# Convolution products moved from GpSimd to ScalarE, and two ScalarE steps placed one ring step sooner

## The reference, cut to what matters

```python
h = rmsnorm(x, norm_mix_pre)
proj = h @ w_in
xr, yr, q, k, v, g_rnn, g_attn = jnp.split(proj, IN_OFFSETS, axis=-1)
# causal depthwise convolution, CONV_WIDTH = 4
xp = jnp.pad(xr, ((0, 0), (3, 0), (0, 0)))
y = conv_b
for k in range(4):
    y = y + xp[:, k:k + S] * conv_w[k]
# recurrence, in 8 blocks of 256 features
r = sigmoid(einsum(y, w_rg_a) + b_rg_a)
i = sigmoid(einsum(y, w_rg_x) + b_rg_x)
log_a = -8.0 * r * softplus(-lru_lambda)
a, mult = exp(log_a), sqrt(-expm1(2.0 * log_a))
h_t = a * h_(t-1) + mult * (i * y)      # an associative scan over time
y_rnn = h * gelu(yr)
y_att = sliding_window_sink_attention(rope(q), rope(k), v, sinks)
```

## Time and profile before

| | |
|---|---|
| median of 3 runs | 2308.87 us (2307.55 to 2314.53) |
| the profiled execution | 2309.7 us, its span 2308.0 us |
| mean granted PE clock | 0.995 of 2.4 GHz |
| PE busy | 2253.3 us, 98% of the span |
| DVE, ACT, POOL busy | 62%, 52%, 17% |

### The profile page before, as it was taken

One profiled execution on the slowest core, in us unless ns is written; L12 is line 12 of the kernel. 1 busy time (PEld: TensorE's weight loads), 2 busy tenths in 40 slices (PEclk: granted clock), 3 DMA queues, 4 the chain that ended last, 5 costly groups with the idle time before them and its releaser, 6 DMA issues.

```text
span 2308.0 us, 32955 instructions
## 1 busy us (share of the span) xinstructions
PE 2253.3 (98%) x11754; PEld 1896.5 (82%) x11754; DVE 1431.4 (62%) x1625; ACT 1195.7 (52%) x1850; POOL 382.0 (17%) x408
## 2 busy tenths in 40 slices
PE   7999999999999999999999999999999999999999
PEld 6888899788888778888888888888977778888887
DVE  6666666654554465555555555566899977675554
ACT  5554456644444446555555555555444446554442
POOL 2134430000000102122121211211233311110000
PEclk9999999999999999999999999999999999999999
DMA  8544444566666856666666666665656665556655
GB/s 246 165 136 136 139 145 147 177 189 192 190 191 193 263 172 188 194 206 203 195 206 204 195 207 199 200 200 163 194 185 187 186 182 166 166 163 191 188 187 163
DMA packets 215028, 427.01 MB, mean 185 GB/s; under 512 B 14033, under 2 KB 14321, under 8 KB 214385
## 3 DMA queue, kind: packets, MB, share of 16 engines
q1 hardware_dynamic: 206720, 398.51, 56.5%
q0 software_dynamic: 7744, 26.62, 3.7%
q10 hardware_dynamic: 432, 0.13, 0.0%
HBM read 414.71 MB, written 10.49 MB: 184 GB/s over the span
## 4 chain that ended last, share of the span: by engine, by line
PE 81%; DVE 11%; ACT 3%; issue 3%; DMA 2%; POOL 1%; SPq 0%; ACTq 0%; DVEq 0%
PE acc L1855 23%; PE acc L1857 22%; PE acc L1856 22%; DVE w_lo L1149 3%; PE acc L1847 3%; PE acc L1849 3%; PE acc L1850 3%; PE tps L1870 1%; DMA raw<-in_w_out_dram 1%; DMA raw<-in_w_in_dram 1%; ACT w_hi L660 1%; POOL k_t L577 1%; PE tps L1976 1%; PE sides L1976 1%; PE sides L1926 1%
## 5 line engine op out<-in xcount | busy, mean ns | idle before, releaser
L1149 DVE TENSOR_TENSOR w_lo<-raw,w_hi 128x1024 fp32r<-128x1024 f32 x752 | 941.4, 1256 | 764.0 <-ACT w_hi L660 759.8
L660 ACT ACTIVATE w_hi<-raw 128x1024 fp32r<-128x1024 f32 x752 | 794.1, 1059 | 904.1 <-PE acc L1857 739.7
L1855 PE MATMUL acc<-w_hi,h_hi 128*128 128x512 f32 x1440 | 572.5, 398 | 5.8 <-DVE w_lo L1149 5.8
L1857 PE MATMUL acc<-w_hi,h_lo 128*128 128x512 f32 x1440 | 562.5, 391 | 0.0
L1856 PE MATMUL acc<-w_lo,h_hi 128*128 128x512 f32 x1440 | 561.8, 390 | 0.0
L1855 PEld LDWEIGHTS acc<-w_hi,h_hi 128*128 128x128 f32 x1440 | 270.7, 188 | 73.1 <-issue 16.8
L1857 PEld LDWEIGHTS acc<-w_hi,h_lo 128*128 128x128 f32 x1440 | 270.6, 188 | 57.4
L1856 PEld LDWEIGHTS acc<-w_lo,h_hi 128*128 128x128 f32 x1440 | 271.1, 188 | 52.9
L1855 PE MATMUL acc<-w_hi,slab_dg_r 128*128 128x512 f32 x768 | 300.5, 391 | 3.6 <-DVE w_lo L1149 3.6
L1856 PE MATMUL acc<-w_lo,slab_dg_r 128*128 128x512 f32 x768 | 299.9, 390 | 0.0
L1857 PE MATMUL acc<-w_hi,slab_dg_r 128*128 128x512 f32 x768 | 299.8, 390 | 0.0
(11 more groups left out here) (370 smaller groups left out, 2314.6 us busy)
## 6 DMA issues: line engine op xcount, KB each, us to landing
raw<-in_w_in_dram SPq DMA_DIRECT2D x328, 512.0 KB, 3.8
raw<-in_w_mlp_up_dram SPq DMA_DIRECT2D x128, 512.0 KB, 3.8
raw<-in_w_mlp_down_dram SPq DMA_DIRECT2D x128, 512.0 KB, 4.7
raw<-in_w_out_dram SPq DMA_DIRECT2D x64, 512.0 KB, 4.6
raw<-in_w_rnn_proj_dram SPq DMA_DIRECT2D x32, 512.0 KB, 3.9
raw<-in_w_attn_proj_dram SPq DMA_DIRECT2D x32, 512.0 KB, 4.8
trig_scratch<-tmp POOLq DMA_DIRECT2D x32, 256.0 KB, 4.4
raw<-in_w_proj_ssm_dram SPq DMA_DIRECT2D x16, 512.0 KB, 3.8
```

Source lines behind the costliest of these rows:

```text
L660: nc.scalar.activation(w_hi[:, j % RING], raw[:, j % RING], ACT.Copy).then_inc(hi_ready, 1)
L1149: V.tensor_tensor(w_lo[:, j % RING], raw[:, j % RING], w_hi[:, j % RING].bitcast(F32), ALU.subtract)\
L1855: T.matmul(o, hi[:, k, c], wh, start=first, stop=False)
L1857: ins = T.matmul(o, lo[:, k, c], wh, start=False, stop=last)
```

## The change

Three things change.

1. ACT makes the scaled copies. A new function `conv_taps(k)` on ACT makes four copies of 128x256 elements per tap, at steps 8, 10, 13 and 13 (`TAPS_AT`) of the attention tables, behind `y_hi` of the same step. Tap 3 writes `slab_d` with the bias, taps 2, 1 and 0 write three buffers `taps[k]`. POOL keeps only the three sums (`conv_sum`).
2. `load_rg(1)` is issued after the last convolution, since its buffers now hold taps until then. `load_rg(0)` stays where it was.
3. In the gelu units ACT's `gates` moves from step 2 to 1 and `decays` from step 3 to 2.

```diff
-        tap = slab_e[:, 8:12, :]
+        taps = [slab_i[:, 12:16, :], slab_e[:, 12:16, :], slab_e[:, 8:12, :]]
...
-                    def conv(c, k):
...
-                        late = 3 - k
-                        if k == 3:
-                            for m in range(QPC):
...
-                                chain.mark(pool.tensor_scalar(slab_d[:, at, :], xr_c[:, m, :], w, b, ALU.mult, ALU.add))
-                            chain.wait()
-                            return
...
-                        chain.link(pool.tensor_tensor(tap[:, :, late:], xr_c[:, :, 0:SEQ - late], w, ALU.mult))
-                        o = slab_d[:, c * QPC:(c + 1) * QPC, late:]
-                        ins = pool.tensor_tensor(o, o, tap[:, :, late:], ALU.add)
+                    def conv_sum(c, k):
+
+                        pool.wait_ge(tap_ready, 4 * c + 4 - k)
+                        o = slab_d[:, c * QPC:(c + 1) * QPC, 3 - k:]
+                        ins = pool.tensor_tensor(o, o, taps[k][:, :, 3 - k:], ALU.add)
...
                     load_rg(0)
-                    pool.wait_ge(tps_ready, NH)
-                    load_rg(1)
-
                     pool.sem_inc(conv_ready, 1)
                     for c in range(NH):
                         normalise(None, c, 0)
                         normalise(None, c, 1)
-                        pool.wait_ge(acc_free[0], c + 2)
-                        conv(c, 3)
                         normalise(None, c, 2)
                         normalise(None, c, 3)
-                        conv(c, 2)
-                        conv(c, 1)
-                        conv(c, 0)
+                        for k in (2, 1, 0):
+                            conv_sum(c, k)
+                    pool.wait_ge(conv_ready, NH + 1)
+                    load_rg(1)
...
+        TAPS_AT = [8, 10, 13, 13]
...
+                def conv_taps(k):
+
+                    if k == 3:
+                        act.wait_ge(acc_free[0], lin(i, 1, c + 2))
+                        act.wait_ge(conv_ready, lin(i, 1, c + 1))
+                    for m in range(QPC):
+                        w = pt1[:, span(i, QPC, COL1["conv_w"] + KT * k + QPC * c + m)]
+                        if k == 3:
+                            b = pt1[:, span(i, QPC, COL1["conv_b"] + QPC * c + m)]
+                            ins = nc.scalar.activation(slab_d[:, span(i, QPC, QPC * c + m), :].rearrange("p o c -> p (o c)"),
+                                                       xr_c[:, m, :], ACT.Identity, scale=w, bias=b)
+                        else:
+                            ins = nc.scalar.activation(taps[k][:, m, 3 - k:], xr_c[:, m, 0:SEQ - 3 + k], ACT.Copy, scale=w)
+                    ins.then_inc(tap_ready, 1)
...
-                return {0: [lambda: gelu(c)], 2: [lambda: gates(c)], 3: [lambda: decays(c)], 4: [lambda: root(c)], 7: [lambda: y_high(c)]}
+                return {0: [lambda: gelu(c)], 1: [lambda: gates(c)], 2: [lambda: decays(c)], 4: [lambda: root(c)], 7: [lambda: y_high(c)]}
```

More of the change, by code:

```diff
@@ L203, in griffin_block_then_ssm_block @@
         conv_ready, rg_done, w_ready = sem("conv_ready"), sem("rg_done"), sem("w_ready")
-        xc_read = sem("xc_read")
+        xc_read, tap_ready = sem("xc_read"), sem("tap_ready")
         d_ready, root_ready, y_ready = sem("d_ready"), sem("root_ready"), sem("y_ready")
@@ L502, in normalise @@
                         ins.then_inc(norm_ready, 1)
-                    def conv(c, k):
-                        late = 3 - k
-                        if k == 3:
-                            for m in range(QPC):
-                                at = c * QPC + m
-                                w = pt1[:, COL1["conv_w"] + KT * k + at:COL1["conv_w"] + KT * k + at + 1]
-                                b = pt1[:, COL1["conv_b"] + at:COL1["conv_b"] + at + 1]
-                                chain.mark(pool.tensor_scalar(slab_d[:, at, :], xr_c[:, m, :], w, b, ALU.mult, ALU.add))
-                            chain.wait()
-                            return
-                        at = COL1["conv_w"] + KT * k + c * QPC
-                        w = pt1[:, at:at + QPC].unsqueeze(2).broadcast_to([P, QPC, SEQ - late])
-                        chain.link(pool.tensor_tensor(tap[:, :, late:], xr_c[:, :, 0:SEQ - late], w, ALU.mult))
-                        o = slab_d[:, c * QPC:(c + 1) * QPC, late:]
-                        ins = pool.tensor_tensor(o, o, tap[:, :, late:], ALU.add)
+                    def conv_sum(c, k):
+                        pool.wait_ge(tap_ready, 4 * c + 4 - k)
+                        o = slab_d[:, c * QPC:(c + 1) * QPC, 3 - k:]
+                        ins = pool.tensor_tensor(o, o, taps[k][:, :, 3 - k:], ALU.add)
                         if k:
@@ L794, in attention @@
                     places += [(at + 1, lambda p=p: exps(p)), (Y_ATT_AT[p] - 1, lambda p=p: pt_copy(p)), (Y_ATT_AT[p], lambda p=p: y_hi(p))]
+                places += [(at, lambda k=k: conv_taps(k)) for at, k in zip(TAPS_AT, (3, 2, 1, 0))]
                 return placed(places, S, 2)[0]
```

## The result

| | before | after |
|---|---|---|
| median of 4 runs | 2309.23 us (2307.55 to 2314.53) | 2291.72 us (2290.99 to 2294.39) |
| the profiled execution | 2309.7 us, span 2308.0 | 2291.69 us, span 2290.0 |

The ratio is 0.9925, with a 95% interval from 0.9911 to 0.9939. The kernel became 17.5 us faster, and the forecast of 2292 us holds. That the medians agree to 0.3 us is partly luck: the changed kernel measured once more, beside the kernel before, was 16.4 us faster.

A forecast was written before the change was run, and what follows sets the result against it. PE, busy 98%, was taken as the bound, losing time to waits on DVE and a slow clock behind them. 12.2 + 4.5 = 16.7 us off 2309.7 gives 2293.0, on the median's scale 2292 us, range 2289 to 2295 (70%).

The forecast's parts named there:

- The rotation: Turn of q after blocks' convolutions: PE's three waits for DVE's last sum (7.3 us) and slow clock (4.9) go, -12.2 us.
- the two meetings of 0.86 us: POOL's three sums behind the last `normalise`: two meet DVE's `w_lo`, each 0.86 us longer, so they end at 123.8 us.
- The spare time: Rotation done at 126.8 us, PE arriving at 128.0 us: PE does not wait, with 1.2 us to spare.
- slow clock: Turn to scores behind each rotation wait: excess of 1.54, 1.72 and 1.63 us at reduced PE clock, 4.9 us in all.
- The gelu and mix units: Earlier gates and decays remove PE's waits for `w_lo` in three gelu units and the first mix unit: -4.5 us.
- the 1.7 us gone in the mix unit: First mix unit: DVE's `decay` starts 1.7 us sooner, so PE's 1.7 us wait for `w_lo` goes.
- the wait goes, in three units: 2.8 us: Gelu units: PE's 0.9 us wait for `w_lo` disappears in each of three units, 2.8 us in all.
- The late load: `load_rg(1)` moved from the start to about 305 us: nothing won at the start, cost 0.
- ACT's copies: 16 copies per block at 0.5 us, 32 us in all on ACT: cost nothing, `pt_copy` done at 118.6 us, covered by 1.3.
- The late rotation: Rival, 15%: POOL's sums still hold DVE's rotation, 1 us of waiting and 1.6 us slow clock three times: 2300 us.
- The gelu rival: Rival, 7%: gelu units win nothing, as the late split of step 3 makes its `w_lo` the next wait: 2296 us.
- its edge of 0.67 us a copy: Rival, 4%: ACT too slow; above 0.67 us a copy, each 0.1 us costs 3.2 us; at 1.5 us, 2319 us.

The follow-up runs named there:

- The kernels with short waits: The changed kernel plus one or two POOL subtractions that read SBUF behind each block's last sum: 2292.30 us with one, 2294.48 us with two.
- its own experiment: The kernel before with only `load_rg(1)` moved behind the last convolution: 2307.83 us, ratio 0.9996 (0.9987 to 1.0006).
- the first reordered kernel: The kernel before with the new gelu places, convolution whole on POOL, taps 3 and 2 ahead of the third `normalise`, tap 1 ahead of the fourth: 2299.93 us.
- part 1 alone: The changed kernel with `gates` and `decays` put back at steps 2 and 3: 2297.09 us, ratio 0.9952 (0.9936 to 0.9969).

## Why the prediction was right, step by step

**The rotation: 12.5 us, forecast 12.2.** The bound was read rightly: DVE's sums were held by POOL's reads, and the experiment with writes against those with reads shows it. The Trainium skill ("SBUF — State Buffer", section "Who interferes with whom") says that a DVE instruction with two SBUF inputs contends with a GpSimd instruction that reads SBUF and not with one that only writes. The runs agree in both halves: 0.42 us beside 5.01 us of memsets, 2.10 us beside a read.

Each time of the working can be checked, with the 0.40 us added by which this trace is early. POOL's sums end at 123.8 (forecast 123.8 to 124.1), with the two meetings of 0.86 us. The first rotation sum is not held, where up to 0.4 us was allowed. The rotation ends at 126.4 (forecast 126.8). PE arrives at 128.04 (forecast 128.0), both counted from the end of its last matmul. The spare time is 1.6 us, not 1.2.

The split between wait and slow clock was not quite right. The excess of 1.54 and 1.72 us from turn to scores was called slow clock. The middle one was put at their mean, 1.63 us, though the same chain has 1.78 us (turn at 191.15, scores at 196.67): of the 0.3 us that the term is short, 0.15 lie there. The kernels with short waits show 0.22 us of the excess at the 2.4 GHz level, so the slow clock itself is 1.3 to 1.6 us. Of the 0.22 us most is a matter of where the chain begins its row: without a wait at the end of the matmul before, 0.17 us behind the first transpose's own start. The sum is not touched by the split, since both parts go with the wait.

**The gelu and mix units: 5.1 us, forecast 4.5.** The chain moved as worked out: gates 3.9 us sooner behind their products, `decay` 1.85 us sooner against the 1.7 forecast, the wait of 0.9 us gone in three units, all but 0.1 of the 1.7 us gone in the mix unit and the two waits that follow still there. The term that was mis-sized is "the wait goes, in three units: 2.8 us". The starts of the gate products are 31.11, 31.11 and 30.99 us apart before, and 29.94, 29.94 and 29.80 after. That is 1.17 or 1.19 us a unit, 3.5 us in all. The wait row's 0.92 us leaves out PE's drain and refill, which the starts above make 0.26 us. The mix unit gave 1.6 us (39.24 to 37.65 from the last gate products), against 1.7: there `decay` comes only 1.60 us sooner behind its products (11.76 instead of 13.36).

The Trainium skill has a formula for each of the two quantities behind this, in "TensorE: Matmul & The Clock Gate". By the section "Single matmul latency" a single bf16 matmul of 256 columns lasts (398 + 256) / 2.4 = 272.5 ns. By the section "Back-to-back issue gap" the gap of isolated matmuls is 256 / 2.4 + 2.5 = 109 ns, while in a stream with weight loads both instructions set the spacing. The rows above, of f32 matmuls in such a stream, have 0.28 and 0.12 us, a little above both. The 0.12 us is measured between starts; the 0.28 us rests on an end that the profile models. The difference of the two is what a row of waits does not count.

**The late load: 0, as forecast**, as far as its own experiment can tell.

**ACT's copies: 0, as forecast.** A copy lasts 0.50 us, exactly the value taken, and tap 3 with its two pointer operands 0.59 us. From start to start it is only 0.40 us. So `pt_copy` was done at 117.59 us, 118.0 with the 0.40 added and 0.6 us sooner than forecast, and the address instructions of the loop cost nothing visible.

**The rivals.** The late rotation did not come, and two extra reads brought it back in a mild form. Its price was put at 1 us of waiting and 1.6 of slow clock each time. At a wait of 0.5 us the clock did not fall at all, nor at the 1.7 to 1.8 us of the first reordered kernel. An estimate from these rows, three times 1 + 0.22 us, puts the case near 2295 us and not at 2300, unless the wait grew to the 2.5 us of before. The gelu rival did not come: the split of step 3 was in time, and no `w_lo` wait is left in the `yr` units. The price of that rival has a slip: 2309.7 - 12.2 is 2297.5 us, and the 2296.7 given is already on the median's scale. The kernel with part 1 alone measured 2297.09 us. ACT was never near its edge of 0.67 us a copy.

## What to carry to other kernels

Look first for DVE instructions with two SBUF inputs on the critical path, and ask when POOL's last read before them ends. That end decides, so issuing POOL's work earlier can be as good as moving it to another engine, but check which small DVE steps it then meets. When PE's wait goes away, price it by the starts of the same work in two units and not by the wait row alone: here a row of 0.92 us was worth 1.17. When one edge of an engine's chain is moved, check the next unit too, since DVE's `decay` one step sooner gave 1.0 us in one place and took it in another.

## What was not expected of the hardware

- The slow clock behind a wait is no fixed price. In three profiles with unchanged convolution PE waits nine times for 2.4 to 2.5 us. Behind eight of these waits the clock was partly at its 1.2 GHz level (granted clock 0.60 to 0.68 over about 4.4 us), and the stretch from turn to scores took 5.28 to 5.54 us. Behind the ninth the granted clock was 1.00 and the stretch took 3.96 us. Waits of 0.5 us, and the three of 1.7 to 1.8 us, left it at 1.00. What decides between the two was not found.
- A DVE instruction of 128x4 elements can be held as long as a large one: 1.56 us instead of 0.17.
- A POOL subtraction with one buffer as both inputs took 1.95 us, and a sum of two buffers on the same number of elements 2.41 us. Whether the buffers or the operation make the difference was not tested.
